# State-space stage of a two-layer trunk: kernel, Toeplitz and carried products on row quarters of a PSUM bank, a blocked scan, Toeplitz transfers issued from two queues

## What is computed

```python
    lam_bar = jnp.exp(lam * dt)
    b_bar = ((lam_bar - 1.0) / lam)[..., None] * b
    bu = jnp.einsum('gpn,bsgn->bsgp', b_bar, uf)
    a = jnp.broadcast_to(lam_bar, bu.shape)
    ...
    _, states = lax.associative_scan(combine, (a, bu), axis=1)
    y = jnp.einsum('gnp,bsgp->bsgn', c, states).real \
        + d_skip.astype(f32).reshape(S5_GROUPS, S5_GROUP_DIM) * uf
    g = jax.nn.gelu(y)
    out = g * jax.nn.sigmoid(g @ w_glu.astype(f32) + b_glu.astype(f32))
```

## Time and profile before

| | us |
|---|---|
| median of 3 timed runs | 1499.51 |
| lowest, highest | 1499.32, 1500.32 |
| profiled execution, its own time | 1503.08 |
| its span in the trace | 1501.4 |

### The profile page before, as it was taken

How to read it: one execution, slowest core, us unless ns; L and a number is a source line. 1 busy time by engine, 2 the same in 40 slices (tenths; PEclk the granted TensorE clock), 3 DMA queues, 4 the chain that set the end, 5 groups by cost and what they waited for, 6 DMA issues and landing times.

```text
span 1501.4 us, 20764 instructions
## 1 busy us (share of the span) xinstructions
PE 1458.6 (97%) x7843; PEld 1229.1 (82%) x7843; DVE 1199.4 (80%) x1235; ACT 975.4 (65%) x949; POOL 115.0 (8%) x136
## 2 busy tenths in 40 slices
PE   7999999999979999999999999999999999999997
PEld 4788799998858888888888888888888888888886
DVE  6983555555885798898898888889989889888987
ACT  4414454444464777877777787777777778777775
POOL 1841300000631000000000000000000000000000
PEclk9999999999999999999999999999999999999999
DMA  8434654443435599999999999999999999999992
GB/s 237 132 50 175 251 212 176 161 141 119 162 113 193 208 361 374 342 358 361 342 358 366 374 333 358 373 334 355 374 337 357 369 373 330 358 376 335 353 377 92
DMA packets 193088, 425.95 MB, mean 284 GB/s; under 512 B 14002, under 2 KB 23088, under 8 KB 192944
## 3 DMA queue, kind: packets, MB, share of 16 engines
q1 hardware_dynamic: 192736, 425.23, 79.2%
q10 hardware_dynamic: 304, 0.06, 0.0%
HBM read 421.67 MB, written 1.05 MB: 282 GB/s over the span
## 4 chain that ended last, share of the span: by engine, by line
PE 90%; DVE 4%; ACT 2%; issue 1%; SPq 1%; POOL 0%; ACTq 0%; DMA 0%; DVEq 0%; POOLq 0%
PE bank L418 75%; PE bank L440 3%; PE bank L865 2%; PE bank L483 2%; DVE w_lo L1760 1%; PE bank L877 1%; PE bank L687 1%; PE bank L522 1%; SPq L1001 1%; PE bank L577 1%; PE bank L663 1%; PE bank L446 1%; PE bank L618 1%; ACT w_hi L1488 0%; PE bank L559 0%
## 5 line engine op out<-in xcount | busy, mean ns | idle before, releaser
L1934 DVE TENSOR_TENSOR w_lo<-ring,w_hi 128x2048 fp32r<-128x2048 f32 x342 | 779.8, 2289 | 101.0 <-ACT w_hi L1488 100.4
L1488 ACT ACTIVATE w_hi<-ring 128x2048 fp32r<-128x2048 f32 x342 | 651.7, 1917 | 127.2 <-PE bank L418 124.2
L418 PE MATMUL bank<-w_hi,xg_hl 128*128 128x512 f32 x1792 | 557.1, 392 | 0.0
L418 PEld LDWEIGHTS bank<-w_hi,xg_hl 128*128 128x128 f32 x1792 | 332.8, 188 | 67.3
L418 PE MATMUL bank<-w_lo,xg_hl 128*128 128x512 f32 x896 | 349.4, 390 | 0.0
L418 PE MATMUL bank<-w_hi,at_hl 128*128 128x512 f32 x896 | 277.5, 391 | 0.0
L418 PEld LDWEIGHTS bank<-w_lo,xg_hl 128*128 128x128 f32 x896 | 168.2, 188 | 35.7
L418 PEld LDWEIGHTS bank<-w_hi,at_hl 128*128 128x128 f32 x896 | 167.0, 188 | 34.0
L418 PE MATMUL bank<-w_lo,at_hl 128*128 128x512 f32 x448 | 174.5, 389 | 0.0
L1810 DVE TENSOR_TENSOR fpart_hl<-ring,fpart_hl 128x1024 fp32r<-128x1024 f32 x66 | 80.6, 1224 | 80.7 <-ACT fpart_hl L1398 80.5
L418 PE MATMUL bank<-ht_hl,fpart_hl 128*128 128x256 f32 x1056 | 130.9, 287 | 2.9 <-DVE work L1853 2.9
(11 more groups left out here) (248 smaller groups left out, 1205.1 us busy)
## 6 DMA issues: line engine op xcount, KB each, us to landing
ring<-in_l_moe_w_gate SPq DMA_DIRECT2D x58, 2048.0 KB, 7.9
ring<-in_l_moe_w_up SPq DMA_DIRECT2D x57, 2048.0 KB, 7.8
ring<-in_l_moe_w_down SPq DMA_DIRECT2D x56, 2048.0 KB, 7.8
ring<-in_l_ffn_w_gate SPq DMA_DIRECT2D x5, 2048.0 KB, 8.8
ring<-in_l_ffn_w_up SPq DMA_DIRECT2D x5, 2048.0 KB, 8.0
ring<-in_l_ffn_w_down SPq DMA_DIRECT2D x5, 2048.0 KB, 7.7
ring<-in_l_w_in SPq DMA_DIRECT2D x4, 2048.0 KB, 8.8
ring<-in_l_w_out SPq DMA_DIRECT2D x4, 2048.0 KB, 8.0
```

The source lines that it names most:

```text
L418: last = mm(p, lhsT=xs[a], rhs=ws[b], start=start and q == 0, stop=stop and q == 2, **kw)
L1488: ac(w_hi(n), at(e_slot(q) * SLOT + j * HALF, HALF), ACT.Copy).then_inc(S("hi"), 1)
L1934: tt(LO[e_slot(q)][:, j * HALF:(j + 1) * HALF], at(e_slot(q) * SLOT + j * HALF, HALF), w_hi(n).bitcast(fp), ALU.subtract).then_inc(S("lo"), 1)
```

## The change

- The kernel products of four pairs stand on rows 0-31, 32-63, 64-95 and 96-127 of a bank, written by width and by real and imaginary part so that four in line have different rows. Four such sets share bank 4, two share bank 5. ACT reads them by row quarter, eight copies instead of six.
- The Toeplitz and carried products of eight pairs share a bank: three banks instead of six. The Toeplitz products stand on four 32-row quarters, the carried ones on two 64-row halves. DVE copies the lower half of each bank, ACT the upper; `y_act` counts ACT's copies.
- The scan has eight blocks of four chunks: powers 1 to 4 of A8 are made (A8P), then three steps inside all blocks at once, then six narrow steps over the last chunks of the blocks, then three steps of seven blocks each that bring the carry to the other three chunks of a block.
- The Toeplitz transfers with g2 = 0 are issued by SP, those with g2 = 1 by ACT.
- mem_keys(0) on PE goes behind the carried products, its ACT copies behind the GELU. DVE's mk0 norm goes behind the scan, its last multiplication behind the copy of the first Y bank.
- POOL clears Tm, then Xbd, ahead of its roots for q0 and mk0.
- The three idle products before yT are gone.

```diff
             for jq in range(6):
-                p = unit(pe, ("K", jq), 4 + jq % 2)
-                for a in range(4):
-                    j = jq * 4 + a
-                    for ri in range(2):
-                        mm(p[0:32, a * P:a * P + GDIM], lhsT=W0bd[:, ri, j], rhs=cT[:, ri, j],
-                           start=(a == 0 and ri == 0), stop=(ri == 1), skip_group_check=True)
...
+                c0 = jq % 4 * P
+                for ri in range(2):
+                    for a in range(4):
+                        mm(kb[jq // 4][32 * a:32 * a + 32, c0:c0 + GDIM], lhsT=W0bd[:, ri, jq * 4 + a], rhs=cT[:, ri, jq * 4 + a],
+                           start=(jq % 4 == 0 and ri == 0), stop=(ri == 1), skip_group_check=True)
+                for ri in range(2):
+                    for a in range(4):
+                        last = mm(kb[jq // 4][32 * a:32 * a + 32, c0 + GDIM:c0 + P], lhsT=W0bd[:, ri, jq * 4 + a],
+                                  rhs=CA[:, ri, jq * 4 + a, 0:7 * GDIM], start=False, stop=(ri == 1), skip_group_check=True)
...
-            yb = [unit(pe, ("Y", n), n) for n in range(6)]
...
+            yb = [unit(pe, ("Y", n), n) for n in range(3)]
+            for n in range(3):
+                for a in range(4):
+                    for jh in range(2):
+                        j = 8 * n + 4 * jh + a
+                        for g2 in range(2):
+                            r0 = 64 * jh + 32 * g2
+                            mm(yb[n][r0:r0 + 32, a * P:(a + 1) * P], lhsT=Ug[:, g2 * PAIRS + j], rhs=Tj[:, g2, j],
+                               start=(a == 0), stop=False, skip_group_check=True)
             pe.wait_ge(S("xbd"), 4)
...
+            mem_keys(0, (4, 5))
+            for n in range(3):
+                pe.wait_ge(S("y_act"), n + 1)
                 read_out(pe, ("Y", n))
...
+        def toeplitz(eng, g2):
+
+            eng.wait_ge(S("kst_d"), 1)
+            eng.wait_ge(S("tm_zero"), 1)
+            Kr, row = Kst.rearrange("p k j o -> p (k j o)"), PAIRS * GDIM
+            for k in range(STEPS):
+                eng.dma_start(Tm[k * GDIM:(k + 1) * GDIM, g2, k * row:STEPS * row],
+                              Kr[g2 * GDIM:(g2 + 1) * GDIM, 0:(STEPS - k) * row]).then_inc(S("tm"), 16)
...
-            for c in range(1, CHUNKS - 1):
-                link(tt(stp, A8, VX[:, :, :, c - 1].unsqueeze(1).to_broadcast([P, 2, 2, PAIRS]), ALU.mult))
-                link(tt(stp[:, :, 0], stp[:, :, 0], stp[:, :, 1], ALU.add))
-                link(tt(VX[:, :, :, c], VX[:, :, :, c], stp[:, :, 0], ALU.add))
...
+            def carry(w_, b0, nb, src, dst):
+
+                t_ = stb[:, :, :, 0:nb]
+                h_ = t_.rearrange("p o (i j) b -> p o i j b", i=2)
+                link(tt(t_, A8P[:, w_].rearrange("p (o ij) -> p o ij", o=2).unsqueeze(3).to_broadcast([P, 2, 2 * PAIRS, nb]),
+                        src.unsqueeze(1).to_broadcast([P, 2, 2 * PAIRS, nb]), ALU.mult))
+                link(tt(h_[:, :, 0], h_[:, :, 0], h_[:, :, 1], ALU.add))
+                d_ = dst.rearrange("p (o j) b -> p o j b", o=2)
+                return link(tt(d_, d_, h_[:, :, 0], ALU.add))
+
+            for r in range(1, SL):
+                carry(0, 0, SB, XB[:, :, :, r - 1], XB[:, :, :, r])
+            for b in range(1, SB - 1):
+                carry(SL - 1, b, 1, XB[:, :, b - 1:b, SL - 1], XB[:, :, b:b + 1, SL - 1])
+            for r in range(SL - 1):
+                carry(r, 1, SB - 1, XB[:, :, 0:SB - 1, SL - 1], XB[:, :, 1:SB, r])
```

More of the change, by code:

```diff
@@ L994, in _ @@
                 if NAMES[n] == "glub":
-                    sp.wait_ge(S("kst_d"), 1)
-                    sp.wait_ge(S("tm_zero"), 1)
-                    Kr, row = Kst.rearrange("p k j o -> p (k j o)"), PAIRS * GDIM
-                    for k in range(STEPS):
-                        for g2 in range(2):
-                            sp.dma_start(Tm[k * GDIM:(k + 1) * GDIM, g2, k * row:STEPS * row],
-                                         Kr[g2 * GDIM:(g2 + 1) * GDIM, 0:(STEPS - k) * row]).then_inc(S("tm"), 16)
+                    toeplitz(sp, 0)
                 if prev:
@@ L1139, in _ @@
             complex_sums(CA, "ca", 12, (ALU.add, ALU.subtract))
+            got(pool, ("V", 2))
+            g.memset(Tm, 0.0).then_inc(S("tm_zero"), 1)
+            g.memset(Xbd, 0.0).then_inc(S("xbd_zero"), 1)
+            for n in range(2):
+                read_out(pool, ("K", n))
+            g.tensor_tensor(Kst[:, 0], Kst[:, 0], MD, ALU.add).then_inc(S("kst_d"), 1)
             root("q0", 1, hss[:, 16:24], hrs[:, 16:24], HD)
             root("mk0", 1, hss[:, 0:8], hrs[:, 0:8], HD)
-            got(pool, ("Bm", 11))
-            g.memset(Xbd, 0.0).then_inc(S("xbd_zero"), 1)
-            got(pool, ("V", 2))
-            g.memset(Tm, 0.0).then_inc(S("tm_zero"), 1)
-            for jq in range(6):
-                read_out(pool, ("K", jq))
-            g.tensor_tensor(Kst[:, 0], Kst[:, 0], MD, ALU.add).then_inc(S("kst_d"), 1)
             root("mk1", 1, hss[:, 8:16], hrs[:, 8:16], HD)
@@ L1292, in _ @@
                 free(ac(dst, src, ACT.Copy), ("V", n))
-            for jq in range(6):
-                p = got(act, ("K", jq))
-                free(ac(Kst[:, :, jq * 4:jq * 4 + 4], p[0:32, :].rearrange("p (a k o) -> p k a o", a=4, k=STEPS), ACT.Copy), ("K", jq))
-            act.wait_ge(S("gp"), 3)
+            for n in range(2):
+                p = got(act, ("K", n))
+                nq = (4, 2)[n]
+                for a in range(4):
+                    j0 = 16 * n + a
+                    last = ac(Kst[:, :, j0:j0 + 4 * nq - 3:4],
+                              p[32 * a:32 * a + 32, 0:nq * P].rearrange("p (q k o) -> p k q o", q=nq, k=STEPS), ACT.Copy)
+                free(last, ("K", n))
             def mem_keys_out(l):
@@ L1708, in _, with power_rows, next_powers @@
             free(last, "q_pw")
+            def power_rows(w0, n):
+                return A8P[:, w0:w0 + n].rearrange("p w (o k j) -> p (w o) k j", o=2, k=2)
+            def next_powers(w0, n, step):
+                m2 = power_rows(step, 1)
+                prods_ = stb.rearrange("p o ij b -> p (o ij b)")
+                t0_, t1_ = (prods_[:, q * 192:q * 192 + n * 96].rearrange("p (r i j) -> p r i j", r=2 * n, i=2) for q in range(2))
+                for k, t_ in enumerate((t0_, t1_)):
+                    last = tt(t_, power_rows(w0, n)[:, :, k].unsqueeze(2).to_broadcast([P, 2 * n, 2, PAIRS]),
+                              m2[:, k].unsqueeze(1).to_broadcast([P, 2 * n, 2, PAIRS]), ALU.mult)
+                link(last)
+                link(tt(power_rows(w0 + step + 1, n), t0_, t1_, ALU.add))
+            for n in range(3):
+                read_out(dve, ("V", n))
+            read_out(dve, "q_pw")
+            next_powers(0, 1, 0)
+            next_powers(0, 2, 1)
+            XB = VX.rearrange("p i j (b r) -> p (i j) b r", r=SL)
+            def carry(w_, b0, nb, src, dst):
[12 more added lines that the diff above has]
+                carry(r, 1, SB - 1, XB[:, :, 0:SB - 1, SL - 1], XB[:, :, 1:SB, r])
+            v.memset(stp[:, 0, 0, 0:1], 0.0).then_inc(S("scan"), 1)
+            dve.wait_ge(S("xbd_zero"), 1)
+            for g2 in range(2):
+                v.tensor_copy(Xbd[g2 * 64:(g2 + 1) * 64, 0, :, g2 * 32 + 1:g2 * 32 + 32],
+                              VX[g2 * 64:(g2 + 1) * 64, 0, :, 0:31]).then_inc(S("xbd"), 1)
             dve.wait_ge(S("ld_hg"), 192)
@@ L1716, in _ @@
             dve.wait_ge(S("s5_ca"), 12)
[L1717 to L1729 removed]
+            head_norm([(heads_of(MKR[0].rearrange("p a b -> p (a b)")), 8)], 8, "mk0", 0, sqk, None)
             def maxima(tag, n, masked, heads):
```

63 lines of the change are left out of this document (29 added, 34 removed).

## The result

| | kernel before | changed kernel |
|---|---|---|
| median of the timed executions, us | 1499.51 (1498.09 to 1501.70, 7) | 1487.29 (1486.16 to 1493.59, 7) |
| profiled execution / its span, us | 1503.08 / 1501.4 | 1486.34 / 1484.6 |
| first GLU product starts, us | 134.29 | 122.54 |

The account below looks back on a forecast made before the run. TensorE's path bounds the kernel, so savings before the first GLU product reach the end: earlier transfers 6.85 + Toeplitz 2.7 + carried 5.35 - clock 2.5 = 12.4 us, from median 1499.51 to 1487.1 us; range 1481 to 1494.

Parts of the forecast that it names:

- Kernel products: PE's kernel products: four row quarters cost the time of one, 12 sets, ending at 86.0 us instead of 95.26.
- rival B: Four row quarters overlap only in pairs: kernel products end at 89.0, saves 8.3 us, total 1491; chance 0.12.
- C: Rival: products on different quarters and halves go one after another; 6 us later than today, total 1506; chance 0.05.
- From there to the transfers: ACT's copies end at 88.9, POOL's clearings at 89.0; Toeplitz transfers start at 90.2, 6.85 us earlier.
- The transfers: Toeplitz transfers queue on the DMA engines, a second issuing queue takes nothing off: 16.9 us, landed at 107.1.
- Rival A: Toeplitz transfers overlap, landing at 100, and the scan becomes the bound: saves 15 to 17.5 us, total 1483; chance 0.15.
- PE meanwhile and the clock: PE finishes memkv1 at 101.0, waits 6.1 us, then runs at low clock: 2.5 us on Toeplitz and carried products.
- The scan: DVE's blocked scan takes 24.5 us from 79.9, ending near 104.4; Xbd is there at 107.1, hidden.
- the meeting with POOL: POOL's add beside the scan holds a DVE operation for 0.90 us instead of 0.23, scan end 105.4 instead of 104.4.
- Behind them: After the carried products: mk0 transposes and copies fit into existing waits, so the 4.24 us to the first GLU product stay.
- Sum: Transfers 6.85 + Toeplitz 2.7 + carried 5.35 - clock 2.5 = 12.4 us saved at the first GLU product.
- rival D: Low clock stretches in later stages come or go: 3 us either way on every case; no chance of its own.

Follow-up runs that it names:

- one_queue: Changed kernel with all 16 Toeplitz transfers issued by SyncE again, in the order of before; median 1487.98 us, ratio 0.9917 to the kernel before.
- swapped_k: Changed kernel with ScalarE's eight Toeplitz transfers in the order k = 1, 0, 3, 2, 5, 4, 7, 6; median 1486.39 us, ratio 0.9909 to before.
- glu_load_last: Changed kernel with the 768 KB GLU weight load held until all 16 Toeplitz transfers have landed; median 1487.01 us, ratio 0.9913 to before.
- half_bytes: Changed kernel with each of the 16 Toeplitz transfers cut to the first half of its row; 1485.31 us (one execution).
- six_banks: Changed kernel with Toeplitz and carried products in six banks on rows 0 to 63 as before, with their copies; median 1496.64 us, ratio 0.9958.

## Why the prediction was right, point by point

**Kernel products.** Right: they ended at 86.07 (forecast 86.0), at the price of one quarter for four. Rivals B and C fall with it. The 2.38 for three column tiles that I had taken from the Trainium skill (TensorE: Matmul & The Clock Gate, Part 3: Packing small matmuls) is for 512 columns; here four took 0.51 us where one had taken 0.51, and the Toeplitz sets 2.83 us for twelve where I had 2.7.

**From there to the transfers.** ACT's copies ended at 89.07 (88.9), POOL's clearings at 88.96 (89.0). The step from there to the first issue was mis-sized: POOL's add took 2.31 us, not about 1.0, since it started inside a DVE operation of 1.6 us. I had charged that meeting to the scan alone. First issue 91.55, not 90.2. The meeting is a matter of chance: of the programs that are the same up to here, one_queue, swapped_k and glu_load_last escaped it and had their first issue at 89.9 to 90.0, as forecast; half_bytes and six_banks didn't. Where the add started just ahead of such an operation (one_queue, glu_load_last) it took 0.99 us and the DVE operation 2.25 and 2.31: the two take turns, and the later one pays.

**The transfers.** Forecast 16.9 us, measured 15.7. I was right that the engines are full and that a second queue gives little: 0.7 us by one_queue. I overlooked the GLU load, which took 1.3 us here and is another transfer behind the same engines. The two errors, 1.35 late and 1.2 short, cancel; the landing at 107.22 (107.1) was luck: with the usual start at 90 the landings were at 105.5 to 106.3. Rival A fell: 15.6 us also with different destinations.

**PE meanwhile and the clock.** memkv1 ended at 100.88 (101.0), then 6.4 us of idle PE and the low clock, as forecast. It lay on the Toeplitz products wholly and not on the carried ones: 5.05 + 5.46 us, against a forecast of 2.7 + 5.3 + 2.5. Sum 10.47 and 10.5.

**The scan.** Forecast 25.5 us with the meeting with POOL, measured 26.6. I took the dearer price an element only in part; less the fixed 158 ns, the measured price is 1.9 ns for the 768-element products and for the last sums of a step. Hidden, as said: Xbd at 108.6, wanted at 112.25. What the prediction didn't say is that the blocks themselves gain so little; its sum never rested on them.

**Behind them.** 4.8 us instead of 4.24. The GLU's first bank is one of the two that the mk0 transposes now use, and waits 0.53 us for ACT's copy of it. I had hidden these copies behind the GLU's first bank, where they are what it waits for.

**Sum.** 11.75 us at the first GLU product, against 12.4: 0.7 too much, almost all from the last point. The medians differ by 12.2. The interval of the ratio, 9.0 to 13.3 us, just shuts out rival B's 8.3; what decides between the two is the timeline. The profiled executions differ by 16.7; the other 5 go with later low stretches (rival D), 27.4 us of them before and 14.2 after. Two of the seven timed executions of the changed kernel took 1493.6: the 3 us that I allowed for this are too few for a single execution, and enough for the median.

## What to carry to other kernels

Small products of 32 or 64 output rows, spread over four quarters or two halves of a bank, cost here what one costs; most of the gain was that. When a wait for a transfer grows because the work ahead of it got shorter, ask what the queue issues next behind that transfer, and whether the idle engine falls to its low clock: both took back part of the gain, and one wait instruction and a few idle products returned it in this stage, by the traces. An operand that steps over memory made an operation here cost 1.7 times as much, so lay out the axis that is to be widened innermost first.

## What the runs showed of the hardware

- **Take turns.** A two-operand product or sum of DVE and one of POOL didn't run at once: 0.99 us of POOL cost a DVE operation 0.7 us, or 1.6 us of DVE held POOL's add for 1.3 us. The Trainium skill (SBUF — State Buffer, Who interferes with whom) says that a VectorE instruction with two SBUF inputs contends with a GpSimd instruction that reads SBUF, that the lock on the shared ports is exclusive, and that issue order decides who blocks; these rows agree, and with the clearings beside the scan, which only write, no DVE operation grew (0.56 us at 87.53).
- **Step between elements.** DVE took 958 ns for 128 x 768 with the inner axis contiguous and 1603 ns with an operand four elements apart; an operand that is repeated along that axis added nothing. The Trainium skill (Vector Engine (DVE) Microarchitecture Reference, 5.2 Measured stream behaviour on trn2) gives 1.05 ns a column for contiguous streams and 1.73 with one source hopping 4 KiB at every element; here it was 1.04, and 1.88 for a hop of four elements, less 158 ns an operation.
- **Landing.** The last transfer was seen as landed 1.7 us after the DMA engines' share had fallen to nothing (102.6 and 104.30 in glu_load_last), and in half_bytes over 2 us.
- **Issuing.** The same eight issues of ScalarE took 11.23 us with full rows and 5.68 with half rows; the last eight of SyncE's sixteen in one_queue took 0.59 us each.
- **The clock.** After 3.1, 3.5, 3.75, 4.65, 5.2, 5.95, 6.4 and 6.9 us of idle PE ahead of the Toeplitz products it was low in them, after 0.23 and 1.55 it wasn't. Ahead of other products it had fallen in the kernel before after 2.10 and 2.87 us and not after 2.76, and in one_queue it hadn't after 2.13 us ahead of the kernel products (1.00 from 81 to 85 us). The idle time alone doesn't decide it, and what does is left open.
